# Paged attention of eight sequences: sequences interleaved, a maximum per partition group joined at the end, and eight pages per step

## The chip, the cores and the metric

The kernel runs on one core of a Trainium2 chip, and its five engines (TensorE, VectorE, ScalarE, GpSimd and SyncE; PE, DVE, ACT, POOL and SP in the profile) work from their own instruction streams. The time is device microseconds of one execution, as the median of several runs. The kernel before takes 2088.8 us, the median of three runs from 2088.06 to 2092.56.

## What is computed

The program is one inference step of a two-layer decoder. The change touches one part of it: the latent attention of the eight sample sequences (`mla_sample`). Each sequence has 4 new tokens and 8 heads, so 32 query rows, and 4096 cached rows of 320 numbers (256 of a latent, 64 of a rotated key). The cache is paged: 32 pages of 128 rows for a sequence, found through a page table.

```python
def mla_sample(h, cache_pool, page_table, w_a, q_norm, wq_b, kv_norm, wkv_b, wo):
    ...
    past = cache_pool[page_table].reshape(b, past_len, MLA_ROW)
    c_past, kr_past = past[..., :KV_LORA], past[..., KV_LORA:]
    q_lat = jnp.einsum('bthd,chd->bthc', q_nope, w_uk)
    s_past = (jnp.einsum('bthc,bkc->bhtk', q_lat, c_past).astype(jnp.float32)
              + jnp.einsum('bthr,bkr->bhtk', q_rope, kr_past).astype(jnp.float32)) * MLA_SCALE
    ...
    p = jax.nn.softmax(jnp.concatenate([s_past, s_new], axis=-1), axis=-1).astype(c.dtype)
    o_lat = (jnp.einsum('bhtk,bkc->bthc', p[..., :past_len], c_past)
             + jnp.einsum('bhtk,bkc->bthc', p[..., past_len:], c))
    o = jnp.einsum('bthc,chd->bthd', o_lat, w_uv).reshape(b, t, MLA_HEADS * V_HEAD)
    ...
    return o @ wo, rows
```

Everything is float32. The rest of the step (the prompt's attention, the sliding-window layer, two expert layers of 32 experts each) is the same in both kernels.

## The kernel before

All waits between engines are semaphores that the code writes by hand: `happened(name, k)` is the count that a semaphore has after k events, `landed` the same for transfers. Each engine's order is the order of its code.

**Pages.** SBUF has two buffers, `pages[0]` and `pages[1]`, each for all 32 pages of one sequence. GpSimd loads the first two sequences early, during the prompt's attention. From then on a sequence b of 2 to 7 goes into the buffer that sequence b - 2 has left. SyncE loads its pages 0 to 15 and GpSimd its pages 16 to 31, one DMA of 160 KB for each page, and both wait for the count of `pv_mm` that says that the matmuls of sequence b - 2 with the values are done:

```python
                    sp.wait_ge(sig["pv_mm"], happened("pv_mm", 2 * i + par - 1))
                    turnstile(sp)
                    load_pages(2 * i + par, par)
```

(here b is `2 * i + par`; GpSimd's loop has the same wait). TensorE waits for both halves, that is for all 32 pages, before its first instruction on a sequence.

**One sequence, `sequence(b, par)`.** Of eight steps, each takes four pages. `keys_T` transposes them on TensorE (`flip`, 12 transposes into PSUM banks 2, 3 and 4), ScalarE and VectorE copy them out into `kT[t % 2]`, and `scores` multiplies them with the queries: 12 matmuls, into four groups of 32 PSUM partitions, each group with its own quarter of the keys. The transposes of step t + 1 stand ahead of the scores of step t. Then come, one behind the other, the scores against the new tokens, a maximum over each partition (VectorE), a transpose of it and a maximum over the four groups, a matmul that spreads it over the partitions, the exponentials (ScalarE), nine transposes of the weights, 33 matmuls with the values (`pv_mm`), three matmuls that add up the four groups, and the division. Only then does TensorE begin with the next sequence. A loop of four passes with two sequences in each runs over the eight.

**Behind it** stand the 16 matmuls that bring all sequences through the value weights (`oTs_mm`), and the projection through `mla_wo` in five row tiles (`wo_mm`, `wo_added`), four of 128 rows and one of 32. `mla_wo` is loaded into `pages[0]` once `pv_mm` says that sequence 6 is done.

## Time and profile before

| | |
|---|---|
| median of three runs | 2088.8 us |
| the profiled execution | 2091.14 us |
| its span in the profile | 2089.3 us |
| TensorE busy | 1741.3 us (83%) |
| VectorE busy | 572.4 us (27%) |
| ScalarE busy | 420.7 us (20%) |
| GpSimd busy | 251.2 us (12%) |
| mean granted TensorE clock | 0.895 |

A busy share counts the time in which an engine has an instruction in work; times within the program are microseconds from the span's start. The clock is given as a share of 2.4 GHz, so that 1.00 is the upper level and 0.50 the lower one, 1.2 GHz. The profiled execution took 2.3 us more than the median.

### The profile page before, as it was taken

The page shows a single profiled execution, that of the slowest core. Times are in us where ns is not written, and L with a number is a line of the kernel's source. Part 1 is how long each engine was busy: PE and PEld are TensorE (multiplying, and loading weights), DVE is VectorE, ACT ScalarE, POOL GpSimd, SP SyncE. Part 2 cuts the span into 40 slices and gives each one's busy share as a digit, 9 for nine tenths or more (in the row PEclk, how much of TensorE's full clock was granted, in tenths as well). Part 3 has the DMA queues.
Part 4 walks back from the last instruction along what each step waited for, and adds up shares of the span by engine and source line. Part 5 has one row for each costly group of instructions (what it writes and reads, how often), then busy time and mean ns, then how long its engine had stood idle before and what let it go on. Part 6 is the DMA issues. An engine that isn't in the chain of part 4 may idle for free.

```text
span 2089.3 us, 31607 instructions
## 1 busy us (share of the span) xinstructions
PE 1741.3 (83%) x10324; PEld 925.6 (44%) x10325; DVE 572.4 (27%) x1554; ACT 420.7 (20%) x854; POOL 251.2 (12%) x349
## 2 busy tenths in 40 slices
PE   6799988888894899888888869999769998888982
PEld 4455565565544343343333334456434444333330
DVE  2233332222204111111111155673321111111114
ACT  2112233333201111111111112432101111111111
POOL 1131002222001111111111120100011111110110
PEclk9999998898896899998999989998879999998896
DMA  3253004555207799999999870000469999999983
GB/s 140 77 140 101 19 4 134 165 146 160 90 0 291 271 408 412 413 410 404 404 410 404 362 272 10 11 7 1 184 274 408 417 413 413 410 404 397 397 360 133
DMA packets 85420, 515.91 MB, mean 247 GB/s; under 512 B 22681, under 2 KB 43098, under 8 KB 59034
## 3 DMA queue, kind: packets, MB, share of 16 engines
q1 hardware_dynamic: 63834, 461.34, 55.4%
q0 software_dynamic: 21536, 53.92, 8.3%
q8 instruction: 29, 0.48, 0.1%
q14 instruction: 21, 0.17, 0.0%
HBM read 508.02 MB, written 26.52 MB: 256 GB/s over the span
## 4 chain that ended last, share of the span: by engine, by line
PE 61%; DMA 24%; DVE 6%; issue 5%; ACT 2%; DVEq 1%; SPq 0%; ACTq 0%; POOLq 0%; POOL 0%
PE ps L1590 52%; DMA mem<-in_moe_w_up 19%; PE ps L1595 10%; DMA moe_rows_in<-mem 2%; DMA mem<-in_x_sample 1%; DVE mem L1334 1%; DMA mem<-in_moe_w_expert 1%; DVE mem L1289 1%; DVE mem L1093 0%; ACT mem L811 0%; ACT mem L771 0%; DVE mem L1405 0%; ACT mem L672 0%; DMA moe_rows_back<-mem 0%; DVE mem L1437 0%
## 5 line engine op out<-in xcount | busy, mean ns | idle before, releaser
L1590 PE MATMUL ps<-mem 128*64 128x512 f32 (+16 forms) x8180 | 1465.7, 460 | 135.8 <-issue 48.5
L1590 PEld LDWEIGHTS ps<-mem 128*64 128x64 f32 (+5 forms) x8180 | 672.2, 148 | 849.9 <-issue 772.0
L1595 PE MATMUL ps<-mem 128*128 128x128 f32 (+5 forms) x2144 | 320.3, 289 | 171.9 <-DVE mem L1289 47.8
L657 ACT ACTIVATE mem<-ps 128x512 f32<-128x512 f32 (+4 forms) x401 | 221.6, 557 | 899.2 <-PE ps L1590 533.0
L1595 PEld LDWEIGHTS ps<-mem 128*128 128x128 f32 (+5 forms) x2144 | 261.0, 168 | 272.4 <-issue 203.4
L1289 DVE TENSOR_TENSOR mem<-mem,ps 64x512 f32<-64x512 f32 x64 | 44.2, 691 | 504.3 <-ACT mem L811 504.3
L586 POOL DMA_INDIRECT mem<-moe_rows_in,mem x70 | 65.1, 930 | 586.7 <-issue 582.1
L1300 DVE COPY mem<-ps 64x512 f32<-64x512 f32 x64 | 44.4, 693 | 307.4 <-PE ps L1590 307.4
L538 POOL DMA_DIRECT2D mem<-in_cache_mla x160 | 85.8, 536 | 327.4 <-issue 327.4
L596 POOL DMA_INDIRECT moe_rows_back<-mem x64 | 59.0, 922 | 353.0 <-DVE mem L1300 346.5
L811 ACT ACT_TABLE_LOAD x32 | 41.1, 1283 | 252.1 <-PE ps L1590 252.1
L811 ACT ACTIVATE mem<-ps 64x512 f32<-64x512 f32 x64 | 37.8, 590 | 200.1 <-PE ps L1590 199.7
L1090 DVE COPY mem<-ps 128x512 f32<-128x512 f32 x64 | 44.3, 692 | 92.7 <-PE ps L1595 90.7
L672 ACT ACTIVATE mem<-mem 128x1024 f32<-128x1024 f32 x25 | 26.4, 1058 | 141.8 <-DVEq L1140 68.6
L847 ACT ACTIVATE mem<-mem 128x256 f32<-128x256 f32 (+1 forms) x64 | 30.3, 474 | 63.1 <-DVEq L1410 63.1
L1294 DVE COPY mem<-ps 128x256 f32<-128x256 f32 x64 | 27.2, 425 | 26.9 <-PE ps L1595 22.9
L1405 DVE CUSTOM_DVE_ANT_0 mem<-ps,mem 128x256 f32<-128x256 f32 (+1 forms) x64 | 26.3, 449 | 27.2 <-PE ps L1590 25.1
L1237 DVE TENSOR_TENSOR mem<-mem 128x320 f32<-128x320 f32 x70 | 33.3, 478 | 0.5 <-issue 0.3
L563 POOL DMA_DIRECT2D mem<-in_moe_b_group x2 | 1.1, 544 | 252.1 <-ACTq L676 252.1
L1334 DVE SCALAR_TENSOR_TENSOR mem<-mem 128x1024 f32<-128x1024 f32 (+1 forms) x20 | 25.6, 1282 | 12.6 <-DMA mem<-moe_rows_back 10.2
L1039 DVE TENSOR_REDUCE mem<-ps 128x1 f32<-128x128 f32 (+3 forms) x32 | 15.7, 490 | 37.7 <-PE ps L1590 37.7
L648 POOL TENSOR_TENSOR mem<-mem 128x1024 f32<-128x1024 f32 (+1 forms) x5 | 12.5, 2510 | 99.4 <-PE ps L1595 99.3
(183 smaller groups left out, 451.7 us busy)
## 6 DMA issues: line engine op xcount, KB each, us to landing
mem<-in_moe_w_gate SPq DMA_DIRECT2D x64, 2048.0 KB, 18.4
mem<-in_moe_w_up SPq DMA_DIRECT2D x64, 2048.0 KB, 22.9
mem<-in_moe_w_down SPq DMA_DIRECT2D x64, 2048.0 KB, 21.1
mem<-in_cache_mla POOLq DMA_DIRECT2D x160, 160.0 KB, 2.7
mem<-in_cache_mla SPq DMA_DIRECT2D x96, 160.0 KB, 2.6
mem<-moe_rows_back SPq DMA_DIRECT2D x8, 1024.0 KB, 8.6
mem<-in_mla_wo SPq DMA_DIRECT2D x1, 4096.0 KB, 13.0
moe_rows_in<-mem POOLq DMA_DIRECT2D x8, 512.0 KB, 15.3
```

The costliest lines, as they stand in the source:

```text
L538: g.dma_start(pages_flat[par][:, bass.ds(j * ROW, ROW)], a["cache_mla"][0][bass.ds(page, 1)].rearrange("a p c -> p (a c)")).then_inc(sig[f ...
L586: g.indirect_dma_start(out=xe[b][0:BLK, :], out_offset=None, in_=rows_in, in_offset=bass.IndirectOffsetOnAxis(ap=fetch_at[b][0:BLK, 0:1].b ...
L596: g.indirect_dma_start(out=rows_back, out_offset=bass.IndirectOffsetOnAxis(ap=store_at[b][0:BLK, 0:1].bitcast(U32), axis=0), in_=ye[b][0:B ...
L657: return act.activation(out, in_, ACT.Copy)
L811: act.activation(sg[BLK:2 * BLK, :], ps[0:BLK, b, :], ACT.Silu).then_inc(sig["silu_ready"], 1)
L1090: v.tensor_copy(kT[t % 2][:, 1], ps[:, 3, :].rearrange("p (g c) -> p g c", g=4)).then_inc(sig["kt1"], 1)
L1237: v.tensor_tensor(onehot[b], rankm[:, :, cols(q, 1)].broadcast_to([P, TILES, BLK]), slots.unsqueeze(1).broadcast_to([P, TILES, BLK]), ALU. ...
L1289: v.tensor_tensor(hid[0:BLK, :], sg[BLK:2 * BLK, :], ps[BLK:2 * BLK, b, :], ALU.mult).then_inc(sig["hid_ready"], 1)
L1300: v.tensor_copy(ye[b][0:BLK, FF:D], ps[BLK:2 * BLK, 2 + b, :]).then_inc(sig["y1_ready"], 1)
L1334: v.scalar_tensor_tensor(out=xt(T, n), in0=ybuf[T][0:n, part * D:(part + 1) * D], scalar=weight[0:n, T:T + 1], in1=xt(T, n), op0=ALU.mult, ...
L1590: return pe.matmul(out, lhsT, rhs, start=start, stop=stop)
L1595: return pe.transpose(out, in_, ident[at:at + n, at:at + n])
```

## The change

- A step takes eight pages: 24 transposes, into banks 2 to 6, and 12 matmuls of 256 columns in the place of 2 x 12 of 128. There are four steps in a sequence. `pages` are taken in another order (`8 * t + ...`), so that a step needs eight pages that follow one another.
- The softmax of sequence b - 1 and its matmuls with the values stand between the steps of sequence b. On TensorE the order is: transposes (b, 0), scores (b - 1, 3), transposes (b, 1), weights (b - 1), scores (b, 0), transposes (b, 2), values (b - 1), scores (b, 1), transposes (b, 3), scores (b, 2).
- Each partition keeps its own maximum (`m_s`) through the exponentials and the values. What the maxima differ by is worked out once behind the last sequence, and goes into `selW`, which 16 matmuls (`oc_mm`) use to add the groups of all sequences. They stand behind the first tile of the projection.
- The scores against the new tokens are worked out once for all sequences, ahead of the first.
- The loop is written out; the queries are read from `qlat` and `qrope` without a copy per sequence.
- SyncE's and GpSimd's code is not edited.

```diff
@@ ScalarE
+            def weigh(b):
+
                 act.wait_ge(sig["nms_ready"], happened("nms_ready", b + 1))
...
+            for b in range(NB):
+                keys_T(b, 0)
+                if b:
+                    weigh(b - 1)
+                keys_T(b, 1)
+                if b:
+                    weights_T(b - 1)
+                keys_T(b, 2)
+                if b:
+                    values(b - 1)
+                keys_T(b, 3)
+            weigh(NB - 1)
@@ VectorE
+            def largest(b):
+
+                v.wait_ge(sig["qk_mm"], happened("qk_mm", 4 * (b + 1)))
+                v.reduce_max(m_s[:, b:b + 1], ps[:, 0:2, :].rearrange("p n c -> p (n c)"), X)
+                v.drain()
+                v.tensor_tensor(m_s[0:NS, b:b + 1], m_s[0:NS, b:b + 1], mn[0:NS, b:b + 1], ALU.max)
+                v.drain()
+                v.tensor_scalar(nm_s[:, b:b + 1], m_s[:, b:b + 1], -MLA_SCALE, None, ALU.mult).then_inc(sig["nms_ready"], 1)
@@ TensorE
+            def keys_T(b, t):
+
+                page, at = pages[b % 2], keys_at(b, t)
+                if t == 0:
+                    if b >= 2:
+                        pe.wait_ge(sig[f"pages{b % 2}"], landed(f"pages{b % 2}", PAGES // 2 * (b // 2)))
+                    pe.wait_ge(sig[f"late_pages{b % 2}"], landed(f"late_pages{b % 2}", PAGES // 2 * (b // 2) + PAGES))
+                for k in range(2):
+                    for half_ in range(2):
+                        bank = 2 + 2 * k + half_
+                        pe.wait_ge(sig[f"tp_ev{bank}"], happened(f"tp_ev{bank}", at if k == 0 else 4 * b + t))
+                        for i in range(4):
+                            last = flip(ps[:, bank, i * P:(i + 1) * P], page[:, 8 * t + 4 * half_ + i, k * P:(k + 1) * P])
+                        last.then_inc(sig[f"tp_mm{bank}"], 1)
+                    pe.wait_ge(sig["tp_ev6"], happened("tp_ev6", ropes_at(b, t) + k))
+                    for i in range(4):
+                        last = flip(ps[0:DR, 6, i * P:(i + 1) * P], page[:, 8 * t + 4 * k + i, CL:ROW])
+                    last.then_inc(sig["tp_mm6"], 1)
...
+                mm(ps[0:NS, 7, 0:CL], pTn[0:NS, :], rowbuf[0:NS, 0:CL], False, True).then_inc(sig["pv_mm"], 1)
...
+            for b in range(NB):
+                keys_T(b, 0)
+                if b:
+                    scores(b - 1, 3)
+                keys_T(b, 1)
+                if b:
+                    weights_T(b - 1)
+                scores(b, 0)
+                keys_T(b, 2)
+                if b:
+                    values(b - 1)
+                scores(b, 1)
+                keys_T(b, 3)
+                scores(b, 2)
+            scores(NB - 1, 3)
+            weights_T(NB - 1)
+            values(NB - 1)
...
+            pe.wait_ge(sig["wo_in"], landed("wo_in", 1))
+            project_out(0)
+            pe.wait_ge(sig["o_s_ready"], happened("o_s_ready", NB))
+            pe.wait_ge(sig["qlat_ready"], happened("qlat_ready", 2))
+            for b in range(NB):
+                for k in range(2):
+                    last = mm(ps[:, 0, (k * NB + b) * NS:(k * NB + b + 1) * NS], o_s[:, b, k * P:(k + 1) * P], selW[:, b, :], True, True)
+            last.then_inc(sig["oc_mm"], 1)
+            project_out(1)
```

Where the work of a sequence's end stands shows best in the rows of each engine's program. TensorE before, from the transposes of one sequence's weights (`128x128 x8` and `32x32`), through the values (`32x256 x33`, the last of which counts `pv_mm`) to the first transposes of the next sequence:

```order
L1595 MATMUL ps<-mem 128x128 x8
L1595 MATMUL ps<-mem 32x32
L1590 MATMUL ps<-mem 32x256 x33
L1590 MATMUL ps<-mem 128x32 x3
L1739 ISA
L1595 MATMUL ps<-mem 128x128 x8
L1595 MATMUL ps<-mem 64x128 x4
```

TensorE now, from the same weights of sequence b - 1 on. In `32x256 x45` the first 33 are the values of b - 1 and the other 12 the scores (b, 1):

```order
L1684 MATMUL ps<-mem 128x128 x8
L1684 MATMUL ps<-mem 32x32
L1679 MATMUL ps<-mem 32x256 x12
L1684 MATMUL ps<-mem 128x128 x8
L1684 MATMUL ps<-mem 64x128 x4
L1684 MATMUL ps<-mem 128x128 x8
L1684 MATMUL ps<-mem 64x128 x4
L1679 MATMUL ps<-mem 32x256 x45
```

Behind these stand 24 more transposes, (b, 3), and 12 matmuls, the scores (b, 2), and then the first instruction on the next sequence, with its waits:

```order
L1684 MATMUL ps<-mem 64x128 [waits tp_ev6]
L1684 MATMUL ps<-mem 64x128 x3
L1679 MATMUL ps<-mem 32x256 [waits tp_ev3,tp_ev2]
L1679 MATMUL ps<-mem 32x256 x3
L1679 MATMUL ps<-mem 32x256 [waits tp_ev5,tp_ev4]
L1679 MATMUL ps<-mem 32x256 x3
L1679 MATMUL ps<-mem 32x256 [waits tp_ev6]
L1679 MATMUL ps<-mem 32x256 x3
L1684 MATMUL ps<-mem 128x128 [waits tp_ev2,late_pages0,pages0]
```

So the matmuls with the values moved from the end of their own sequence into the third step of the next one, and between them and the wait for a new sequence's pages there are now two steps of scores and one of transposes, where a whole sequence stood before.

ScalarE now, around the exponentials of sequence b - 1 (`L798`, `128x1024`); ahead of them are the three copies of step (b, 0), behind them the three of step (b, 1), and then the copy of the transposed weights. Before, the exponentials had no copies of keys behind them that TensorE waited for:

```order
L679 ACTIVATE mem<-ps 128x512 [waits tp_mm4]
L798 ACTIVATE mem<-ps,mem 128x1024 [waits nms_ready]
L800 ACTIVATE mem<-mem 32x32
L679 ACTIVATE mem<-ps 128x512 [waits tp_mm2,qk_mm]
L679 ACTIVATE mem<-ps 64x512 [waits tp_mm6]
L679 ACTIVATE mem<-ps 128x512 [waits tp_mm4]
L679 ACTIVATE mem<-ps 128x512 [waits pv_mm,tp_mm2]
```

The copy of bank 6 (`64x512`), which the second half of TensorE's 64-row transposes needs, moved behind the exponentials.

## Rows read from the trace of the kernel before

**Rows 1.** The chain that ended last, by engine, from the page.

```profile
PE 61%; DMA 24%; DVE 6%; issue 5%; ACT 2%; DVEq 1%; SPq 0%; ACTq 0%; POOLq 0%; POOL 0%
```

**Rows 2.** The page's slices of 52 us: GB/s that the DMA engines moved.

```profile
GB/s 140 77 140 101 19 4 134 165 146 160 90 0 291 271 408 412 413 410 404 404 410 404 362 272 10 11 7 1 184 274 408 417 413 413 410 404 397 397 360 133
```

**Rows 3.** Timeline (start, duration, engine, line, tiles, idle before): first transposes, last values, projection.

```profile
286.67 4.42 PE L1595 MATMUL ps<-mem 128*128 128x128 f32 x24 [2.98 <-DVEq L1080]
...
554.11 5.22 PE L1590 MATMUL ps<-mem 128*32 128x256 f32 x66
...
561.66 69.11 PE L1590 MATMUL ps<-mem 128*128 128x32 f32 x192 [0.99 <-DVEq L1122]
```

**Rows 4.** Windows, one for each sequence: busy times, granted clock, DMA share, GB/s.

```profile
core 0: us, PE busy (x) PEld busy (x) DVE busy (x) ACT busy (x) POOL busy (x), PEclk, DMA share, GB/s
286.60:320.30 33.70, 29.49 (x374) 20.95 (x374) 8.85 (x18) 11.59 (x22) 0.00 (x0) 0.85 0.01 2
320.30:354.40 34.10, 28.95 (x380) 20.12 (x380) 9.85 (x23) 11.94 (x22) 8.58 (x16) 0.90 0.54 155
```

**Rows 5.** Timeline of one four-page step.

```profile
326.10 1.53 PE L1595 MATMUL ps<-mem 128*128 128x128 f32 x12
326.80 0.60 ACT L657 ACTIVATE mem<-ps 128x512 f32<-128x512 f32 x1 [0.93 <-PE ps L1595]
327.23 0.69 DVE L1090 COPY mem<-ps 128x512 f32<-128x512 f32 x1 [1.70 <-PE ps L1595]
327.56 1.00 PE L1590 MATMUL ps<-mem 128*32 128x128 f32 x24
327.67 0.59 ACT L657 ACTIVATE mem<-ps 64x512 f32<-64x512 f32 x1 [0.28 <-PE ps L1595]
328.49 1.53 PE L1595 MATMUL ps<-mem 128*128 128x128 f32 x12
```

**Rows 6.** Timeline of a sequence's end, from the maximum to the values.

```profile
307.90 1.23 DVE L1093 TENSOR_REDUCE mem<-ps 128x1 f32<-128x1024 f32 x1 [2.19 <-PE ps L1590]
...
309.29 0.15 DVE L1096 TENSOR_TENSOR mem<-mem 32x1 f32<-32x1 f32 x1
...
311.27 1.11 ACT L771 ACTIVATE mem<-ps,mem 128x1024 f32<-128x1024 f32 x1 [5.23 <-DVE mem L1105]
...
312.81 2.13 PE L1595 MATMUL ps<-mem 128*128 128x128 f32 x9 [1.76 <-ACTq L775]
...
314.87 5.38 PE L1590 MATMUL ps<-mem 128*32 128x256 f32 x66
```

**Rows 7.** GpSimd's page DMAs: an early one, then first and last of later loads.

```profile
99.95 0.54 POOL L538 DMA_DIRECT2D mem<-in_cache_mla  x1 [0.99 <-issue]
...
321.92 0.54 POOL L538 DMA_DIRECT2D mem<-in_cache_mla  x1 [43.70 <-issue]
...
346.63 0.54 POOL L538 DMA_DIRECT2D mem<-in_cache_mla  x1 [1.10 <-issue]
356.40 0.54 POOL L538 DMA_DIRECT2D mem<-in_cache_mla  x1 [9.24 <-issue]
...
383.60 0.54 POOL L538 DMA_DIRECT2D mem<-in_cache_mla  x1 [1.26 <-issue]
...
519.90 0.54 POOL L538 DMA_DIRECT2D mem<-in_cache_mla  x1 [1.26 <-issue]
```

**Rows 8.** The 96 page DMAs of line 538 from 280 to 600 us.

```profile
DMA to landing us min/median/max: 2.4/2.8/4.1
```

**Rows 9.** Windows of short stretches, columns as in rows 4.

```profile
286.70:290.00 3.30, 3.30 (x16) 3.14 (x17) 0.69 (x1) 1.10 (x2) 0.00 (x0) 0.50 0.00 0
290.00:292.00 2.00, 2.00 (x35) 1.41 (x34) 0.69 (x1) 1.27 (x3) 0.00 (x0) 1.00 0.00 0
...
317.30:320.20 2.90, 2.90 (x46) 1.20 (x38) 0.00 (x0) 0.00 (x0) 0.00 (x0) 1.00 0.00 0
```

**Rows 10.** The page's DMA issues: KB, us from issue to landing.

```profile
mem<-in_mla_wo SPq DMA_DIRECT2D x1, 4096.0 KB, 13.0
```

More of the change, by code:

```diff
@@ L235, in build @@
         rowbuf = m.take(ROW)
+        cq_at = m.at
         cq = m.take(QL)
@@ new lines, in _ @@
+            for G in range(4):
+                v.tensor_copy(lg_s[0:NS, G], l_s[G * NS:(G + 1) * NS, :])
+            v.drain()
+            v.tensor_tensor(lg_s[0:NS, 0], lg_s[0:NS, 0], ln_s[0:NS], ALU.add)
+            v.drain()
+            v.tensor_tensor(lg_s[0:NS], lg_s[0:NS], dg[0:NS], ALU.mult)
+            v.drain()
+            v.tensor_reduce(lt_s[0:NS], lg_s[0:NS].rearrange("p g b -> p b g"), X, ALU.add)
+            v.drain()
+            v.reciprocal(lt_s[0:NS], lt_s[0:NS])
+            v.drain()
@@ L1784, in sequence, with values @@
+            def values(b):
+                page, at = pages[b % 2], weights_at(b)
                 pe.wait_ge(sig["o_s_ready"], happened("o_s_ready", b))
-                pe.wait_ge(sig["pTa_s"], happened("pTa_s", b + 1))
-                for t in range(8):
-                    if t == 4:
-                        pe.wait_ge(sig["pTb_s"], happened("pTb_s", b + 1))
+                pe.wait_ge(sig["tp_ev2"], happened("tp_ev2", at + 1))
+                for i in range(8):
+                    if i == 4:
+                        pe.wait_ge(sig["tp_ev3"], happened("tp_ev3", at + 1))
@@ L1796, in sequence @@
-                for k in range(2):
-                    mm(ps[:, 5, 256 + k * NS:256 + (k + 1) * NS], o_s[:, k * P:(k + 1) * P], sel32, True, True)
-                mm(ps[:, 5, 320:320 + NS], l_bc, sel32, True, True).then_inc(sig["oc_mm"], 1)
-            with pe.Fori(0, NB // 2) as i:
-                for par in range(2):
-                    sequence(2 * i + par, par, i)
-            pe.wait_ge(sig["olat_ready"], happened("olat_ready", NB))
-            for hh in range(H):
-                for k in range(2):
-                    last = mm(ps[:, 0, hh * NS:(hh + 1) * NS], wkvb[:, k, (2 * hh + 1) * DN:(2 * hh + 2) * DN], olatT[:, k, hh, :],
-                              k == 0, k == 1)
@@ L1808, in _ @@
-            last.then_inc(sig["oTs_mm"], 1)
-            pe.wait_ge(sig["wo_in"], landed("wo_in", 1))
-            for T in range(TILES):
+                        mm(ps[G * NS:(G + 1) * NS, 7, 0:CL], pT_s[:, i, G * NS:(G + 1) * NS],
+                           page[:, 8 * (i // 2) + 2 * G + i % 2, 0:CL], i == 0, i == 7 and G > 0)
+                pe.wait_ge(sig["tp_ev6"], happened("tp_ev6", new_weights_at(b) + 1))
+                mm(ps[0:NS, 7, 0:CL], pTn[0:NS, :], rowbuf[0:NS, 0:CL], False, True).then_inc(sig["pv_mm"], 1)
```

320 lines of the change are left out of this document (171 added, 149 removed).

## The prediction

> **What bounds the kernel now.** I read the chain of work that ended last first: TensorE holds 61% of it and DMA 24% [rows 1]. The GB/s slices say where the DMA part is: near 410 in the expert layers, but 134 to 165 in slices 7 to 10, where the pages of the eight sequences are loaded [rows 2]. The part that the change touches runs from 286.67 us, the first transposes, to 559.33 us, the end of the last values (554.11 + 5.22) [rows 3]: 272.7 us for eight sequences. One takes about 34.1 us (from 320.30 to 354.40), with TensorE busy for 28.95 us of it and DMA for 0.54 [rows 4]. So TensorE's own order sets the time. A step of four pages takes 2.39 us (328.49 - 326.10): 12 transposes until 327.56, that is 1.46 us or 0.122 us each, and 24 passes of scores in 0.93 us (a float32 matmul shows as two passes). The copies of ScalarE and VectorE, 0.60, 0.59 and 0.69 us, lie beside it [rows 5]. Behind the steps comes the serial end: the maximum starts at 307.90, the exponentials at 311.27, the transposes of the weights at 312.81, the values at 314.87, and these end at 320.25 [rows 6].
>
> The second thing to see is when the pages travel. GpSimd's first DMA for sequence 2 is issued at 321.92, 1.7 us after the values of sequence 0 end at 320.25; the next one for sequence 3 at 356.40 [rows 6, 7]. The last of the sixteen stands at 346.63 in the first case and at 383.60 in the second, so 24.7 and 27.2 us of issue; over all six loads (the last issue is at 519.90) the mean of my readings is 26.3 us, and a page lands 2.8 us after its issue at the median [rows 7, 8]. From the end of the values of sequence b - 2 until all pages of b are there I count L = 1.8 + 26.3 + 2.8 = 30.9 us. Before, TensorE has the whole of sequence b - 1 to do in that time, 34.1 us, so L is hidden with some 3 us to spare. That cover is what the change takes away.
>
> **The change, part by part.**
>
> *Where the values stand.* They now come in the third step of the next sequence, and SyncE's and GpSimd's code still waits for them before it loads into the buffer. Between the values of b - 1 and the first instruction of b + 1, which needs every page of the load that they start, TensorE has only the scores (b, 1), the transposes (b, 3) and the scores (b, 2). So the period is L plus S, where S is what TensorE does from the arrival of the pages to the end of the next values.
>
> *The unit costs.* 24 transposes at full clock: 24 x 0.122 = 2.92 us. The scores of a step are 24 passes of 256 columns. No row has exactly these. In the values, passes of 256 columns take 2.90 / 46 = 0.063 us at full clock [rows 9]; two four-page score steps take 2 x 0.93 = 1.86 us. The bounds are 1.5 and 1.86 us, and I take 1.7. The values, 66 passes at full clock, take about 4.4 us (they took 5.38 with their first part at the lower clock) [rows 6]. Nine transposes of weights take 1.1 us at full clock and 2.1 at the lower one (312.81 to 314.87).
>
> *The clock.* When the first transposes begin at 286.67, TensorE has been idle, and its granted clock is 0.50 for 3.3 us of work, then 1.00; 16 transposes fit into the 3.3 us, 0.21 us each [rows 9]. After each wait of some 24 us for pages the same will happen: transposes (b + 1, 0) take 16 x 0.23 + 8 x 0.122 = 4.6 us in the place of 2.92.
>
> *The new stall.* ScalarE has its copies of step (b + 1, 1) behind the exponentials of b. After the scores (b, 3) come the maximum and two small operations, 1.7 us (1.23, 0.15, 0.15 and their gaps), the exponentials, 1.54 us (311.27 to 312.81), and then two copies, 0.60 and 0.59 us [rows 5, 6]: 4.5 us until bank 6 is free. TensorE has 20 transposes to do by then, 2.43 us, and waits for 2.15 us (gaps of the semaphores included). VectorE's copies, 0.69 us, are ready earlier.
>
> *S, in order:* transposes (b + 1, 0) 4.6; scores (b, 3) 1.7; 20 transposes 2.43; stall 2.15; four transposes 0.49; weights 1.1; scores (b + 1, 0) 1.7; transposes (b + 1, 2) 2.92; values 4.4. The sum is 21.5 us, and 0.4 us more for the chance that the clock falls again in the stall, so 21.9 us. The period is 30.9 + 21.9 = 52.8 us where it was 34.1.
>
> *What is gained.* With the pages there in time, a period is 4 x 2.92 + 4 x 1.7 + 1.1 + 4.4 + 2.15 = 26.1 us: the serial end is gone from TensorE's path, some 8 us in each sequence. That gain exists only for the first two sequences, whose pages were loaded long before.
>
> *The sum.* From the first transposes: new-token scores 1.7 us; sequence 0 without its end 4.6 + 3 x 2.92 + 3 x 1.7 = 18.5; S without the slow clock, 19.8, until the values of sequence 0: at 40.0 us. Six periods of 52.8 us: 316.8. After the values of sequence 6: scores (7, 1), transposes (7, 3), scores (7, 2) and (7, 3) 8.0; maximum and exponentials 3.3; weights 2.1; values 5.3: 18.7. Together 375.5 us against 272.7, so +102.8 us.
>
> *The rest I cost at nothing.* Sixteen small copies and the copies per sequence go (some 1.5 us, once), and the new scores come in their place. Behind the last values, 32 passes of `oc_mm` are added (about 4 us at a transpose's 0.122 us each), and the wait of 2.3 us from 559.33 to the first project-out work at 561.66 goes, with the slow clock behind it [rows 3]. VectorE's chain that joins the maxima, about a dozen operations of 0.15 us, lies beside the first tile of the projection, which takes over 10 us of the 69.11 that 32 passes like those and all five tiles have [rows 3]; without that cover it would cost 3 us. `mla_wo` is loaded from the end of the values of sequence 6, 18.7 us before it is needed, and travels for 13 us [rows 10].
>
> The profiled execution took 2091.1 us and would take 2193.9; the median lies 2.3 us lower, so I forecast 2192 us.
>
> **The rule I weighed.** Transposes alone brought the clock from 0.50 to 1.00 at 290 us, before any other matmul of the part [rows 9]. The Trainium skill, "TensorE: Matmul & The Clock Gate", section "Part 4: PE-mode transpose", says that transposes don't count as busy work for the clock gate, so that it does not open in transpose mode. By that rule the transposes behind each wait would stay at the lower clock, which is the third rival; the trace speaks against it.
>
> **The rivals.**
>
> *The pages are hidden anyway (faster).* Then a period is 26.1 us, the part takes 40.0 + 6 x 26.1 + 18.7 = 215.3 us, and the kernel 2031 us. It needs the pages to land within 6.3 us of the values (26.1 - 19.8); the sign changes where L is 34.1 - 21.9 = 12.2 us. That is 5.24 MB in about 8 us of transfer, over 600 GB/s, where no slice shows over 417 [rows 2]. And the issue alone takes 24.7 us. It would take a wait of TensorE that I have misread. 5%.
>
> *Neither (no change).* It needs L near 12 us, and nothing points there. 2%.
>
> *The transposes stay at the lower clock (slower still).* 72 transposes of each period at 0.23 us are 16.6 us in the place of 10.4, and the weights 1.0 us more: 7.1 us for six periods, and about 14 us in the first two sequences and the last. That gives 2249 us. 5%.
>
> *The forecast.* 88%.
>
> **How the numbers follow.** L could fall: GpSimd's early loads were issued every 0.54 + 0.99 = 1.53 us [rows 7]; sixteen at that pace take 23.0 us, so L = 27.6, and 20 us less in all. The stall could be hidden and the scores be at their lower bound: 3 us less per period, 18 us. Upwards, the long loads throughout give 5 us, a clock that falls in each stall 8 us, and gaps at each of the seven waits of a step some 2 us per period, 12 us. All of one sign together is unlikely: I take 2160 to 2222. That leaves out both far rivals and a little of the forecast. A measurement of this kernel tells about 0.2%, 4 us, from no change: faster 0.05, same 0.02, slower 0.93.
>
> **What the new profile would show.** GpSimd's page DMAs should come in groups about 53 us apart from their start, with the same 1.65 to 1.8 us between two. TensorE should be idle for some 24 us (30.9 less the 6.3 of the work in between) before the first transposes of sequences 2 to 7, and the wait be put down to DMA; its clock should be 0.50 for the first 3 to 4 us behind. Sequences 0 and 1 should run faster than before, with the values of sequence 0 ending 40 us behind the first transposes. A stall of about 2 us should stand before the last four transposes of step (b + 1, 1), with the release from ScalarE. The expert layers should be as before. The prediction is wrong if the pages' wait is short, by a DMA issue that is much faster beside an idle TensorE, or if TensorE's work comes out well over 22 us per period.

## The result, and the profile after

The changed kernel takes 2193.0 us (median of four runs, 2191.04 to 2197.13), the kernel before 2088.4 us on the same chip (four runs, 2086.43 to 2092.56): a ratio of 1.0501, with a 95% interval of 1.0478 to 1.0523. It is 5% slower. The profiled execution took 2191.04 us with a span of 2189.4 us, and the mean granted TensorE clock fell from 0.895 to 0.869.

The page of the kernel after: engines; the clock and the GB/s in 40 slices, now of 54.7 us; the chain by engine; the load of `mla_wo`. They answer to [rows 1, 2, 10].

```profile
PE 1728.2 (79%) x9464; PEld 910.6 (42%) x9465; DVE 582.0 (27%) x1523; ACT 398.7 (18%) x823; POOL 251.7 (11%) x349
...
PEclk9999987777779779999899898999869999898886
...
GB/s 136 95 138 86 3 26 115 99 96 98 104 130 0 226 241 411 407 411 407 403 410 408 395 285 263 1 15 3 1 292 384 411 414 413 410 401 396 405 365 128
...
PE 58%; DMA 21%; issue 7%; SPq 5%; DVE 5%; ACT 2%; DVEq 1%; ACTq 0%; POOLq 0%; POOL 0%
...
mem<-in_mla_wo SPq DMA_DIRECT2D x1, 4096.0 KB, 13.2
```

TensorE is busy for 13 us less than before (1728.2 for 1741.3) in a span 100 us longer: time in which it waits was added. The slices place it. Slices 7 to 12 (328 to 657 us), where the pages travel, show about 100 GB/s and a clock of 0.7; the expert layers behind them reach 414 GB/s, as they reached 417 before.

TensorE's timeline with the first matmul of the part, a whole period and most of the next (columns as in [rows 3]):

```profile
278.35 3.17 PE L1679 MATMUL ps<-mem 128*128 128x32 f32 x12 [1.25 <-DVEq L1127]
...
322.97 1.64 PE L1679 MATMUL ps<-mem 128*32 128x256 f32 x24
347.74 4.55 PE L1684 MATMUL ps<-mem 128*128 128x128 f32 x24 [23.13 <-DMA mem<-in_cache_mla]
352.22 1.64 PE L1679 MATMUL ps<-mem 128*32 128x256 f32 x24
353.79 2.40 PE L1684 MATMUL ps<-mem 128*128 128x128 f32 x20
358.43 1.63 PE L1684 MATMUL ps<-mem 128*64 128x128 f32 x13 [2.23 <-ACT mem L679]
359.99 1.64 PE L1679 MATMUL ps<-mem 128*32 128x256 f32 x24
361.56 2.84 PE L1684 MATMUL ps<-mem 128*128 128x128 f32 x24
364.33 5.78 PE L1679 MATMUL ps<-mem 128*32 128x256 f32 x90
370.04 2.84 PE L1684 MATMUL ps<-mem 128*128 128x128 f32 x24
372.81 1.64 PE L1679 MATMUL ps<-mem 128*32 128x256 f32 x24
400.32 5.35 PE L1684 MATMUL ps<-mem 128*128 128x128 f32 x24 [25.88 <-issue]
405.60 1.77 PE L1679 MATMUL ps<-mem 128*32 128x256 f32 x24
407.31 2.40 PE L1684 MATMUL ps<-mem 128*128 128x128 f32 x20
411.94 2.18 PE L1684 MATMUL ps<-mem 128*64 128x128 f32 x13 [2.23 <-ACT mem L679]
414.05 2.60 PE L1679 MATMUL ps<-mem 128*32 128x256 f32 x24
416.58 2.84 PE L1684 MATMUL ps<-mem 128*128 128x128 f32 x24
419.35 5.78 PE L1679 MATMUL ps<-mem 128*32 128x256 f32 x90
```

How to read it: `x90` is 66 passes with the values and 24 of scores behind them, so the values end 1.57 us before the group: at 368.5 and at 423.56 us. After them come two groups, 24 transposes and 24 passes of scores, and then TensorE stands idle: 23.13 us, 25.88 us, and in the four waits that follow 25.19, 25.43, 22.99 and 25.37 us, together 148.0 us. One of the six is put down to DMA and five to "issue". The next table shows that these are the same wait. GpSimd's page DMAs (columns as in [rows 7]), first and last of two loads:

```profile
320.38 0.54 POOL L560 DMA_DIRECT2D mem<-in_cache_mla  x1 [48.90 <-issue]
...
345.12 0.54 POOL L560 DMA_DIRECT2D mem<-in_cache_mla  x1 [1.11 <-issue]
370.56 0.54 POOL L560 DMA_DIRECT2D mem<-in_cache_mla  x1 [24.90 <-issue]
...
397.75 0.54 POOL L560 DMA_DIRECT2D mem<-in_cache_mla  x1 [1.26 <-issue]
```

All 96 of them, from issue to landing, as in [rows 8]:

```profile
DMA to landing us min/median/max: 2.3/2.8/4.2
```

A load begins 1.6 to 2.0 us after the values, its last DMA is issued 24.7 to 27.2 us later, and TensorE begins 2.6 us after that (347.74 - 345.12; 400.32 - 397.75), in the wait labelled DMA and in the one labelled "issue" alike. The loads start at 320.38, 370.56, 425.21, 479.77, 534.35 and 586.28 us, 53.2 us apart at the mean.

Windows of the kernel after (columns as in [rows 4]): the first part until the values of sequence 0 end, two periods, then short stretches.

```profile
278.30:318.70 40.40, 38.12 (x379) 28.69 (x383) 18.02 (x35) 13.79 (x26) 0.00 (x0) 0.90 0.01 1
318.70:368.60 49.90, 24.54 (x272) 17.19 (x275) 10.22 (x17) 9.19 (x19) 8.60 (x16) 0.76 0.37 106
368.60:423.60 55.00, 26.89 (x271) 18.22 (x271) 10.32 (x17) 9.14 (x18) 8.60 (x16) 0.72 0.34 96
...
347.70:351.00 3.30, 3.26 (x16) 3.14 (x17) 0.69 (x1) 1.03 (x2) 0.00 (x0) 0.50 0.01 2
...
400.30:404.20 3.90, 3.88 (x19) 3.75 (x20) 0.69 (x1) 1.39 (x3) 0.00 (x0) 0.50 0.00 0
404.30:405.50 1.20, 1.20 (x7) 0.81 (x5) 0.64 (x1) 0.30 (x1) 0.00 (x0) 0.50 0.05 14
408.00:412.00 4.00, 1.77 (x17) 1.53 (x16) 2.29 (x5) 2.69 (x7) 0.00 (x0) 1.00 0.00 0
...
414.00:416.60 2.60, 2.60 (x26) 0.81 (x25) 0.78 (x2) 0.00 (x0) 0.00 (x0) 0.58 0.00 0
```

In a period of 50 to 55 us TensorE is now busy for 25 to 27, where it was busy for 28.95 of 34.1 before [rows 4]: the change does make a sequence cheaper in work, and the page transfer, 0.54 of the DMA engines' time before, fills 0.34 to 0.37 of a longer one.

The end of a sequence's scores, where the small stall stands (as [rows 6]; weight loads left out):

```profile
407.44 1.22 DVE L1143 TENSOR_REDUCE mem<-ps 128x1 f32<-128x1024 f32 x1 [1.05 <-PE ps L1679]
...
409.16 1.11 ACT L798 ACTIVATE mem<-ps,mem 128x1024 f32<-128x1024 f32 x1 [4.55 <-DVE mem L1147]
...
410.81 1.55 ACT L679 ACTIVATE mem<-ps 128x512 f32<-128x512 f32 x3 [0.16 <-issue]
```

ScalarE's first two copies of step (b + 1, 1) come behind the exponentials and end at 411.9, where TensorE's last four transposes begin (411.94, idle 2.23 us, released by ScalarE's line 679).

Before, the part took 272.7 us from its first transposes; now, from 278.35 to 657.6 us (the end of the last values), 379.3 us.

### The profile page after: what moved, and what is told of

Its sections match the earlier page's. It is cut to its first block, busy times and chain, and to the rows that moved or that the text cites. A ratio compares the mean times of both kernels' runs of the same rounds, so it can differ in the third digit from the quotient of the medians.

```text
span 2189.4 us, 29196 instructions
## 1 busy us (share of the span) xinstructions
PE 1728.2 (79%) x9464; PEld 910.6 (42%) x9465; DVE 582.0 (27%) x1523; ACT 398.7 (18%) x823; POOL 251.7 (11%) x349
## 4 chain that ended last, share of the span: by engine, by line
PE 58%; DMA 21%; issue 7%; SPq 5%; DVE 5%; ACT 2%; DVEq 1%; ACTq 0%; POOLq 0%; POOL 0%
PE ps L1679 49%; DMA mem<-in_moe_w_up 16%; PE ps L1684 9%; SPq L420 2%; SPq L421 2%; DMA moe_rows_in<-mem 1%; SPq L419 1%; DMA mem<-in_x_sample 1%; DMA mem<-in_cache_mla 1%; DVE mem L1423 1%; DMA mem<-in_moe_w_expert 1%; DVE mem L1378 1%; ACT mem L859 0%; DVE mem L1143 0%; ACT mem L798 0%
## 5 line engine op out<-in xcount | busy, mean ns | idle before, releaser
L1679 PE MATMUL ps<-mem 128*64 128x512 f32 (+15 forms) x7328 | 1447.6, 494 | 120.6 <-issue 48.6
L1679 PEld LDWEIGHTS ps<-mem 128*64 128x64 f32 (+4 forms) x7328 | 647.4, 152 | 833.8 <-issue 757.4
L1684 PE MATMUL ps<-mem 128*128 128x128 f32 (+3 forms) x2136 | 320.6, 295 | 300.1 <-issue 124.9
L1684 PEld LDWEIGHTS ps<-mem 128*128 128x128 f32 (+3 forms) x2136 | 270.2, 172 | 403.4 <-issue 313.4
L679 ACT ACTIVATE mem<-ps 128x512 f32<-128x512 f32 (+4 forms) x369 | 199.0, 552 | 1029.5 <-PE ps L1679 528.2
L1389 DVE COPY mem<-ps 64x512 f32<-64x512 f32 x64 | 44.4, 693 | 311.6 <-PE ps L1679 311.6
L1383 DVE COPY mem<-ps 128x256 f32<-128x256 f32 x64 | 27.2, 425 | 27.0 <-PE ps L1684 23.0
L1494 DVE CUSTOM_DVE_ANT_0 mem<-ps,mem 128x256 f32<-128x256 f32 (+1 forms) x64 | 26.3, 448 | 27.5 <-PE ps L1679 25.4
L1138 DVE COPY mem<-ps 64x512 f32<-64x512 f32 x32 | 21.7, 677 | 15.7 <-PE ps L1684 15.5
```

The costliest lines, as they stand in the source:

```text
L679: return act.activation(out, in_, ACT.Copy)
L1389: v.tensor_copy(ye[b][0:BLK, FF:D], ps[BLK:2 * BLK, 2 + b, :]).then_inc(sig["y1_ready"], 1)
L1679: return pe.matmul(out, lhsT, rhs, start=start, stop=stop)
L1684: return pe.transpose(out, in_, ident[at:at + n, at:at + n])
```

## Experiments

Each ratio is to the kernel before, run beside it on the same chip. Three chips were used, with the kernel before at 2092.4, 2091.3 and 2095.6 us. Differences between two kernels are given from the medians, and where the chips differ also from the ratios.

**No loads for the later sequences.** The changed kernel, without the page DMAs of sequences 2 to 7:

```diff
@@ SyncE
                     turnstile(sp)
-                    load_pages(2 * i + par, par)
@@ GpSimd
                     turnstile(g)
-                    load_pages(2 * i + par, par, PAGES // 2)
@@ TensorE, keys_T
-                    if b >= 2:
-                        pe.wait_ge(sig[f"pages{b % 2}"], landed(f"pages{b % 2}", PAGES // 2 * (b // 2)))
-                    pe.wait_ge(sig[f"late_pages{b % 2}"], landed(f"late_pages{b % 2}", PAGES // 2 * (b // 2) + PAGES))
+                    pe.wait_ge(sig[f"late_pages{b % 2}"], landed(f"late_pages{b % 2}", PAGES))
```

> The changed kernel without the page loads of sequences 2 to 7: SyncE and GpSimd issue none of them, and those sequences are worked out from the pages that sequences 0 and 1 have in the two buffers, so that their part of the output leaves their own cache out. Everything on TensorE, ScalarE and VectorE is as in the changed kernel. Theory (the pages' load stands on TensorE's path): the period falls from 53.4 us to what TensorE does, 26.1 us by my sum (28 at most, by the steps of the changed kernel's first two sequences), and the whole to about 2033 us (2025 to 2045). Rival (the written-out loop, instruction fetch or the new order of copies costs the time): the kernel stays above 2150 us. Rival (half and half): between.

2031.9 us (2028.76 to 2034.98), ratio 0.9711 (0.9691 to 0.973). This measures what TensorE's work takes without any wait for later pages; the forecast's rival for hidden pages said 2031. Two periods of this kernel in windows:

```profile
320.00:348.20 28.20, 25.97 (x272) 17.45 (x275) 10.22 (x17) 9.17 (x19) 0.00 (x0) 0.88 0.01 2
348.20:374.70 26.50, 24.27 (x271) 16.29 (x274) 10.22 (x17) 9.06 (x19) 0.00 (x0) 0.94 0.00 1
```

Over these and the next two, a period takes 28.2, 26.5, 28.0 and 26.3 us, the longer ones at a lower clock, for 26.1 us forecast. The lower clock stands behind the stall of 2.23 us, which this kernel has too, and once lasts through the next transposes:

```profile
334.92:343.90 8.98, 8.98 (x61) 6.31 (x61) 2.43 (x5) 2.81 (x5) 0.00 (x0) 0.62 0.00 0
444.01:449.90 5.89, 5.89 (x61) 4.45 (x61) 2.47 (x5) 2.70 (x5) 0.00 (x0) 1.00 0.01 3
```

Both windows hold the same work, from the end of the stall to the values: 3.1 us more at the lower clock. All of the loss against this kernel, 161 us (2193.0 - 2031.9), comes with the page loads: six periods longer by 53.4 - 27.2 us give 157.

**Half of the pages.** Eight pages per queue and sequence are loaded, in the place of sixteen:

```diff
-                with sp.Fori(0, PAGES // 2) as j:
+                with sp.Fori(0, PAGES // 4) as j:
...
-                    load_pages(2 * i + par, par, PAGES // 2)
+                    load_pages(2 * i + par, par, PAGES // 2, 3 * PAGES // 4)
...
-                        pe.wait_ge(sig[f"pages{b % 2}"], landed(f"pages{b % 2}", PAGES // 2 * (b // 2)))
-                    pe.wait_ge(sig[f"late_pages{b % 2}"], landed(f"late_pages{b % 2}", PAGES // 2 * (b // 2) + PAGES))
+                        pe.wait_ge(sig[f"pages{b % 2}"], landed(f"pages{b % 2}", PAGES // 4 * (b // 2)))
+                    pe.wait_ge(sig[f"late_pages{b % 2}"], landed(f"late_pages{b % 2}", PAGES // 4 * (b // 2) + PAGES))
```

> The changed kernel with half of the page loads of sequences 2 to 7: SyncE and GpSimd load 8 pages each in the place of 16, and the other 16 pages keep what the buffer had, so that output leaves them out. Theory (period = load + TensorE's work behind it): eight issues fewer on each queue, 8 x 1.73 = 13.8 us off every one of the six periods, so 53.4 becomes 39.6 us and the kernel takes 2193 - 83 = 2110 us (2103 to 2118). Rival (the wait has a large fixed part, such as the landing of the last page or the start of the loop): much less than half of the load's 26 us goes, and the kernel stays above 2140 us. Rival (part of the load is hidden by something that I count twice): the slope is less than one, 2120 to 2140 us.

2102.6 us (2101.11 to 2102.98), ratio 1.0046 (1.003 to 1.0062). From the third to the fourth sequence TensorE's wait is now this:

```profile
374.60 5.36 PE L1684 MATMUL ps<-mem 128*128 128x128 f32 x24 [11.44 <-issue]
```

11.44 us in the place of 25.88. The loads start some 39.5 us apart where it was 53.2, so the period follows the issue of the pages one to one: eight DMAs per queue fewer, 13.7 us less. A kernel limited by TensorE's own order would not have moved. The time lies just under the 2103 to 2118 us expected: of the 88 us between the two profiles (spans of 2189.4 and 2101.2 us), 83.3 lie ahead of the expert layers, and the other 5 behind them, in code that no edit touches.

**The other parts of the change without the interleaving.** The eight-page steps and the maxima per partition stay, but each sequence runs to its end before the next, on all engines:

```diff
@@ TensorE
             for b in range(NB):
                 keys_T(b, 0)
...
+                for t in range(3):
+                    keys_T(b, t + 1)
+                    scores(b, t)
+                scores(b, 3)
+                weights_T(b)
+                values(b)
```

> The changed kernel with one part of the change undone: the sequences don't interleave. Steps of eight pages, the maximum for each partition and the join at the end stay; weights and values of a sequence stand behind its own four steps, as before. Theory (the interleaving alone costs the time, because it moves the release of the buffer next to the need for it; the other parts gain): between the values of b - 1 and the pages of b + 1 there is a whole sequence of work again. TensorE's own period is 4 x (2.92 + 1.7) + 3.3 + 2.1 + 5.3 = 29.2 us, and the load is 30.6 us, so the load just about binds and the period is 30.6 to 31.5 us: the part takes about 8 x 31 = 248 us in the place of 273, and the kernel about 2065 us (2055 to 2078). Rival (eight-page steps or the copies' new places cost time by themselves): not faster than the kernel before, 2085 us or more.

2065.9 us (2057.73 to 2067.06), ratio 0.9863 (0.984 to 0.9887): faster than before by 1.4%. Two waits for pages in it:

```profile
373.14 5.69 PE L1680 MATMUL ps<-mem 128*128 128x128 f32 x48 [1.70 <-issue]
...
498.87 7.43 PE L1680 MATMUL ps<-mem 128*128 128x128 f32 x48 [7.10 <-issue]
```

From the first transposes of sequence 1 to those of sequence 7 a sequence takes 30.9 us at the mean (313.30 to 498.87), as expected. The waits for pages in it are 0.98, 1.70, 0.36, 3.28, none and 7.10 us, so the load still binds, but only just. The long last wait has a cause of its own: the load of `mla_wo` was issued at 491.81 us, beside the last pages, and the last of these, issued at 492.86, took 5.9 us to land in the place of 2.8. So the larger steps and the joined maxima together gain; the interleaving is what costs. This run takes all of it back, on every engine; that the moment at which the buffer is released counts by itself, the next two runs show.

**The kernel before, with its loads held back.** In the old kernel, the loads for a sequence now wait until half of the scores of the sequence between are done:

```diff
                     turnstile(sp)
+                    sp.wait_ge(sig["qk_mm"], happened("qk_mm", 8 * (2 * i + par - 1) + 4))
+                    turnstile(sp)
                     load_pages(2 * i + par, par)
...
                     turnstile(g)
+                    g.wait_ge(sig["qk_mm"], happened("qk_mm", 8 * (2 * i + par - 1) + 4))
+                    turnstile(g)
                     load_pages(2 * i + par, par, PAGES // 2)
```

> The kernel before, with one wait more on SyncE and GpSimd: the pages of sequence b are not loaded before TensorE has done four of the eight steps of sequence b - 1, some 12 us after the values of b - 2. No other line is changed. Theory (slack of about 3 us, and beyond it every us of lateness is paid): the load starts 11.5 us later and binds, the period is 12.8 + 29.5 = 42.5 us plus 1.5 us of slow clock behind the wait, in the place of 34.1, for six sequences: 2088 + 60 = 2148 us (2130 to 2160). Rival (the load has much more room than I read, since the page loads would run faster in one burst beside a waiting TensorE): under 2110 us.

2145.0 us (2144.61 to 2145.34), ratio 1.0251 (1.0231 to 1.0272). A late release alone, with nothing else of the change, slows the old kernel by 52.6 us and gives it a wait that it did not have:

```profile
362.93 5.36 PE L1599 MATMUL ps<-mem 128*128 128x128 f32 x24 [7.28 <-DMA mem<-in_cache_mla]
```

**Values one step earlier.** In the changed kernel, only on TensorE:

```diff
                 scores(b, 0)
-                keys_T(b, 2)
                 if b:
                     values(b - 1)
+                keys_T(b, 2)
                 scores(b, 1)
```

> The changed kernel with one block moved on TensorE: the values of b - 1 stand ahead of the transposes (b, 2) instead of behind them. Theory (period = load + TensorE's work behind the pages, up to the values): the buffer is released 2.8 us earlier in each period, and those 2.8 us of transposes move into the wait for pages. The period falls from 53.4 to 50.6 us, the kernel to 2193 - 17 = 2176 us (2168 to 2182). Rival (the total of TensorE's work counts, and its order does not matter): 2190 us or more. Rival (the values now wait for the copies of their weights): some 1 us of the gain per period goes, 2182 us.

2173.6 us (2172.93 to 2174.59), ratio 1.0393 (1.037 to 1.0416). The load starts 24 transposes earlier relative to the need, 2.77 us by the rows above, 16.6 us for six periods. From one wait's end to the next it is 49.9 us (348.54 to 398.43) in the place of 52.6, and the kernel came down by 19 us (2193.0 - 2173.6), by the two ratios 23 us. What stands in front of the release counts in full, as the sum L + S says.

**Waits by the step.** The pages are loaded in four groups of eight (SyncE takes the first four of a group, GpSimd the others), each counted by its own semaphore, and TensorE waits at each step for that step's pages only:

```diff
+                for t in range(4):
+                    with sp.Fori(8 * t, 8 * t + 4) as j:
...
+                                     ).then_inc(sig[STEP_SIG["s"][par][t]], DMA)
...
+                if b >= 2:
+                    name = STEP_SIG["s"][b % 2][t]
+                    pe.wait_ge(sig[name], arrived(name, 4 * (b // 2)))
```

> The changed kernel with the pages waited for step by step: SyncE loads pages 0 to 3 and GpSimd pages 4 to 7 of each group of eight, every group has semaphores of its own, and TensorE waits in each step only for its own eight pages. The order of TensorE's work is that of the changed kernel, the bytes and the count of DMAs are the same. Theory (what costs is that all 32 pages must be there before the first step): the first group is there 1.8 + 3 x 1.73 + 2.8 = 9.8 us behind the values instead of 30.6; TensorE has 6 us of work by then, waits 4 us, some 2 us more for the second group and hardly at all behind it. Period about 31 us, kernel about 2193 - 6 x 22.4 = 2059 us (2048 to 2075), faster than the kernel before. Rival (the load as a whole, 27 us of issue, plus the work that must follow its last page binds): over 2100 us.

2065.8 us (2057.57 to 2069.39), ratio 0.9884 (0.986 to 0.9907). The wait breaks up into shorter ones ahead of single steps:

```profile
332.20 4.21 PE L1703 MATMUL ps<-mem 128*128 128x128 f32 x24 [3.91 <-DMA mem<-in_cache_mla]
...
339.91 2.38 PE L1703 MATMUL ps<-mem 128*128 128x128 f32 x20 [1.92 <-issue]
```

The edit changed one thing more. GpSimd's loop over sixteen pages became four loops over four, and the sixteen DMAs of sequences 3, 5 and 7 now go out in 24.6 us (354.98 to 379.58 for sequence 3) where they took 27.1 to 27.2. Those of 2, 4 and 6 take 0.5 to 0.9 us longer than before. This was not forecast; it is at most some 8 of the 127 us gained.

**Both: values one step earlier and waits by the step.**

> Both edits together: values of b - 1 ahead of the transposes (b, 2), and pages waited for in groups of eight. Theory: TensorE has 8.8 us of work between the values and the first group (there after 9.8 us), waits 1 us for it and 2 us for the second; the period comes to 28 to 29.5 us, where the issue of sixteen pages per queue (27.7 us) begins to bind. Kernel about 2193 - 6 x 24.5 = 2046 us (2036 to 2056). Rival (by 31 us per period the queues bind already): no better than the run with step waits alone, 2055 us or more.

2039.2 us (2037.78 to 2042.64), ratio 0.9755 (0.9735 to 0.9774), 52 us faster than the kernel before with all pages loaded. One period of it, as a timeline:

```profile
328.10 2.81 PE L1703 MATMUL ps<-mem 128*128 128x128 f32 x24 [1.23 <-DMA mem<-in_cache_mla]
...
335.29 3.95 PE L1703 MATMUL ps<-mem 128*128 128x128 f32 x33 [2.81 <-DMA mem<-in_cache_mla]
...
355.44 2.81 PE L1703 MATMUL ps<-mem 128*128 128x128 f32 x24 [1.81 <-issue]
...
390.81 5.48 PE L1703 MATMUL ps<-mem 128*128 128x128 f32 x33 [3.36 <-issue]
```

A period is 27.3 us (355.44 - 328.10), and 27.6 at the mean of five. TensorE now waits only for 0.6 to 3.4 us at a time. In the period shown the clock stayed up: 24 transposes behind the wait took 2.81 us, where they took 4.1 to 5.4 us behind the longer waits of the changed kernel and of the one with waits by the step. It did not in every period: behind the second wait, the same 33 transposes took 3.95 us twice and 5.48 us three times (the last row). By the ratios this kernel lies 9 us above the one without any page load (0.9755 and 0.9711 of 2090 us) and 23 us below the serial order (0.9863). These 23 us are not the interleaving's alone: the serial kernel still waits for its pages as one block, 13.4 us in all, and issues its loads for three of the sequences 2.5 us slower. A serial order with waits by the step was not run, so what the interleaving itself is worth beside it stays open.

**Work to keep the clock up, 184 transposes.** To price the clock by itself, the wait is filled with transposes of the identity into unused columns:

```diff
                 scores(b, 2)
+                if 1 <= b < NB - 1:
+                    for _ in range(184):
+                        flip(ps[:, 7, 384:512], ident)
```

> The changed kernel with 184 transposes of the identity behind the scores (b, 2) of sequences 1 to 6, into 128 unused columns of PSUM bank 7: about 22.5 us of work at full clock that fills the wait for pages, and whose result nobody reads. Theory (of the 53.4 us, 2 to 3.5 are the slow clock behind the wait): the transposes of the first step take 2.84 instead of 4.6 to 5.4 us and the clock falls less in the stall; the period shrinks by 2 to 3.5 us and the kernel to 2193 - 12 to 21 = 2172 to 2181 us. Rival (the clock's part is nothing, the pages set everything): 2191 us or more. If the filler ran past the pages' arrival it would cost time, and the kernel would be slower than 2195 us.

2193.0 us (2186.85 to 2195.83), ratio 1.0485 (1.0456 to 1.0514). This expectation was missed. The rows say why:

```profile
327.99 20.31 PE L1684 MATMUL ps<-mem 128*128 128x128 f32 x184
351.09 4.48 PE L1684 MATMUL ps<-mem 128*128 128x128 f32 x24 [2.79 <-DMA mem<-in_cache_mla]
...
405.05 5.14 PE L1684 MATMUL ps<-mem 128*128 128x128 f32 x24 [5.52 <-issue]
```

The filling took 20.31 us, 0.110 us each, and left gaps of 2.8 and 5.5 us, after which the transposes were as slow as without it (4.48 and 5.14 us). Filling most of a wait brought nothing that could be told (by the two ratios 3 us). If the lower clock comes from the gap that is left, a filling without one must bring more; the next run tries that.

**The same, filled to the end.**

```diff
-                    for _ in range(184):
+                    for _ in range(204 if b in (1, 5) else 226):
```

> The run with filler transposes again, with the filler long enough: 184 of them took 20.31 us and ended 2.8 to 5.5 us before the pages, so here 204 stand behind the scores (b, 2) of sequences 1 and 5 and 226 behind those of 2, 3, 4 and 6 (0.110 us each), and end within about 1 us of the pages. Theory (the slow clock behind the wait is part of the 53.4 us): transposes (b + 1, 0) take 2.84 us where the changed kernel has 4.55 to 5.36, so 2.3 us less per period on average, with or without a fall in the stall: kernel 2193 - 14 = 2179 us (2172 to 2184). Rival (the clock has no part, or filler and pages disturb each other): 2189 us or more.

2176.5 us (2171.57 to 2177.37), ratio 1.0389 (1.0359 to 1.0419).

```profile
374.74 24.89 PE L1684 MATMUL ps<-mem 128*128 128x128 f32 x226
400.63 2.81 PE L1684 MATMUL ps<-mem 128*128 128x128 f32 x24 [1.00 <-issue]
```

With a gap of 1.00 us, the transposes behind it take 2.81 us in the place of 5.35, and start 25.9 us behind the start of the filling (400.63 - 374.74), which is as long as the wait was: the pages come no earlier. Keeping the clock up is thus worth about 16 to 23 us (2193.0 - 2176.5; by the two ratios, 0.0112 of 2090 us), about a fifth of the loss of 105 us. Some 14 us of it are the six groups of transposes behind the waits (30.6 us in the changed kernel, 16.4 here, each counted to the start of the scores behind it); the rest fits the stalls, behind which the clock fell in two of six periods here and in five of six there. What remains of the loss is the wait itself.

**Copies ahead of the exponentials.** On ScalarE, two of the three copies of step (b, 1) stand before the exponentials of b - 1:

```diff
                 keys_T(b, 0)
+                keys_T(b, 1, last=False)
                 if b:
                     weigh(b - 1)
-                keys_T(b, 1)
+                keys_T(b, 1, first=False)
```

> The changed kernel with two of ScalarE's copies moved: the copies of banks 2 and 6 of step (b, 1) stand ahead of the exponentials of b - 1, the copy of bank 4 behind them. Theory (TensorE's 2.23 us stall in each sequence is the bank 6 copy queued behind the exponentials, and the clock falls in it): the last four transposes of the step no longer wait; the weights wait about 0.9 us for the later exponentials instead. 1.3 to 1.4 us less in seven sequences, and in the ones where the clock fell in the stall up to 1.5 us more: kernel 2193 - 10 to 18 = 2175 to 2183 us. Rival (the exponentials are what TensorE waits for in either order): 2190 us or more.

2173.1 us (2170.31 to 2180.43), ratio 1.0383 (1.0358 to 1.0408), 2 us under the range expected, on the side of the theory. The 2.23 us stall is gone and a shorter one stands in its place, for the weights, released by the exponentials:

```profile
411.90 1.22 PE L1691 MATMUL ps<-mem 128*128 128x128 f32 x9 [0.78 <-ACTq L808]
```

Behind this shorter stall the clock did not fall in any period: the nine transposes took 1.22 or 1.23 us each time. In the changed kernel the thirteen behind the stall took 1.63 us at full clock and 2.05 to 2.66 us in the other five periods.

**All three edits together** (values earlier, waits by the step, copies first).

> The run with both page edits (values of b - 1 ahead of the transposes (b, 2), pages waited for in groups of eight) and ScalarE's two copies ahead of the exponentials. Theory (in that run the pages of the second and third group bind in sequences 2 to 7, the stall only in the first two and the last): 1.4 us less in one or two sequences and a little where the clock no longer falls: 2039 - 3 to 8 = 2031 to 2036 us. Rival (TensorE's own work still binds in all of them): 1.4 us and more off each of seven sequences, 2029 us or less.

2037.3 us (2033.46 to 2046.22), ratio 0.9724 (0.97 to 0.9747), 1 us above the range expected. The interval overlaps that of the kernel with two of the edits (0.9735 to 0.9774): no gain of the third could be told here. Either of the two is the fastest version found, 2.5 to 2.8% faster than the kernel before.

## Why the prediction was right, step by step

The forecast of 2192 us, and its mechanism, held: 2193.0 us.

*L, from the values to the pages.* Forecast 1.8 + 26.3 + 2.8 = 30.9 us. Measured over the six loads: 1.75 + 26.3 + 2.5 = 30.6 us. The issue did not become faster beside an idle TensorE. The 24.7 and 27.2 us stood in [rows 7] and stand in the kernel after again. One sign was wrong: the wait was to be put down to DMA, and the profile does so in one of six cases.

*S, from the pages to the values.* Forecast 21.9, measured 22.8 us at the mean (20.8 in the first period, 22.9 to 23.4 in the others). This is the term that was mis-sized. In the period from 400.32 to 423.56: the transposes behind the wait took 5.28 us for 4.6; the scores (b, 3) 1.71 for 1.7; 20 transposes 2.40 for 2.43; the stall 2.23 for 2.15; four transposes and the weights 2.11 for 1.59; the scores (b + 1, 0) 2.53 for 1.7; the next transposes 2.77 for 2.92; the values 4.21 for 4.4. The sum is 23.24. What was too small was the clock, twice. Behind the wait I took the 3.3 us at 0.50 of [rows 9]; once it was about that (347.70 to 351.00), but in the other five periods the transposes took 5.12 to 5.36 us, and the windows show 0.50 up to 405.5 us in the one read. And I gave 0.4 us to a fall of the clock in the stall, as a chance; it fell in five of six periods (0.58 from 414.00 to 416.60), and cost 1.5 us there (4.64 us from 411.94 to 416.58, for the work that took 3.13 from 358.43 to 361.56). Two slips worked the other way and hid part of this. The unit costs at full clock were read a little high (24 transposes 2.77 us for 2.92, the scores of a step 1.57 for 1.7), and a slow transpose was put at 0.23 us, where the row read for it gives 0.21 and the kernel after 0.22 (5.28 / 24).

*The sum.* The values of sequence 0 ended 40.4 us behind the start (forecast 40.0); six periods took 320.2 us (316.8); the end 18.7 us (18.7). Together 379.3 us for 375.5, so +106.6 us for +102.8.

*The rest at nothing.* From the last values to the end of the projection it took 71.0 us (657.6 to 728.64) where it was 71.4 (559.33 to 630.77): `oc_mm` and the vanished wait cancel, as costed. The next work of TensorE, the router's, waits for a transfer in both kernels and began 82.5 us behind the last values in the place of 81.9. VectorE's chain for the maxima was to lie beside the first tile of the projection; it ran earlier, from 652.39 to 655.70 us, beside the last values, and cost nothing.

*What was not forecast.* The part began at 278.35 us and not at 286.67 [rows 3], 8.3 us earlier. The removed copies give 1.6 us between the 16 transposes before the part and its first matmul; the other 6.7 us arose upstream, in code that the change doesn't edit. Those 16 transposes began between 270.2 and 273.9 us in every profiled kernel with the change's code, and at 276.9 and 277.0 us in the two without it. So it is more than one execution's doing, but the profiled one, at 270.2, is the earliest of the eleven. Nothing was tried on it, and its cause is open. It hid the 3.8 us by which the part was under-estimated. That the total came within 1 us of the forecast is therefore luck in part: the two profiled executions differ by 99.9 us, the medians by 104.6, and the forecast was 103.2.

*The rivals.* "The pages are hidden anyway" fell: 23 to 26 us of waiting stand in each of six periods. But its price was right: 2031 us forecast, 2031.9 us for the kernel without the loads. That it agrees within 1 us is luck too: its periods took 27.2 us for 26.1, and its part began 7.6 us earlier than before (279.10 for 286.67 us). "The transposes stay at the lower clock" fell as well. In the filled wait of the ninth experiment 226 transposes with nothing else ran at 0.110 us each, and this window of them shows the granted clock:

```profile
376.00:399.00 23.00, 23.00 (x213) 23.00 (x212) 0.00 (x0) 0.00 (x0) 6.99 (x13) 1.00 0.65 185
```

By the Trainium skill, "TensorE: Matmul & The Clock Gate", section "Part 4: PE-mode transpose", transposes don't count as busy work for the clock gate in the way that matmuls do, and it doesn't open for them; here they alone held the clock at 1.00 for 23 us, so for these float32 transposes the measurement decides against the rule. That the rise behind five of the six waits came only at about the end of the 24 transposes would, taken alone, also fit the rule.

*The cause.* It rests on edits in both directions: the late release alone, put into the old kernel, cost 52.6 us; the whole change without its interleaving gained 26.5 us; without the loads it gained 60.5 us; moving the values alone by one step took 19 us off the changed kernel; with half of them the period fell by the issue time left out; and with the wait divided by steps the change was 1.2% faster than before in the place of 5% slower, 2.5% with the values one step earlier too.

## What to carry to other kernels

When work is interleaved across iterations, look at the last use of each buffer: moving it later moves the start of the next load, and the distance from that use to the next need must stay above the load's whole time, issue of every DMA included (here 30.6 us against some 6). If the distance can't be kept, divide the wait: one count per step's pages gave back more than the change had lost. And a long activation in front of copies that TensorE needs makes a short stall, which here cost 2.2 us and, through the clock behind it, 1.5 us more in most periods (in the kernel without the loads up to 3.1).

## What the runs showed of the hardware

- A gap of 2.2 us in TensorE's work was followed by a lower clock in five of six periods of the changed kernel (0.63 over the 4.6 us behind it in each of the five, 1.00 in the sixth), and not in the stall of sequence 1 ahead of them. In the kernel with waits by the step a gap of 3.06 us was followed by 33 transposes at full clock (3.95 us), and in the one with both edits gaps of 2.45 and 2.81 us were, but gaps of 2.08, 2.86 and 3.36 us by the same 33 in 5.48 us. Gaps up to 1.0 us were never followed by the slow pace in the filled kernel. So from 2 to 3 us a gap's length alone did not decide, and what did is open.
- GpSimd's loop of page DMAs had two paces: 1.65 us from one to the next in the loads for sequences 2 and 6, 1.80 us in those for 3, 5 and 7, both before and after, whether TensorE worked or stood. The load for sequence 4 went at 1.65 to 1.77 us with one step of 3.5 us in the middle. In the kernels whose loops take four pages, the slow pace of 3, 5 and 7 is gone (24.6 us for their sixteen in the place of 27.1 to 27.2), so it hangs on the loops and not on the sequence: on their code, or on which pages of a sequence GpSimd takes, which that edit changed too. The two were not tried apart. SyncE's loop went at 1.6 us for sequences 2 and 3 alike. The two queues so move 5.24 MB in 27 to 30 us.
- A wait labelled "issue" can be one for DMA: five of the six waits for pages were labelled so, and ended 2.4 to 2.6 us behind the last page's issue, as the one labelled DMA did.
